# Spectral stages of a Hyena encoder on one Trainium2 core: bins 0 and N1/2 of each request group computed in one step from 64 kept values each, instead of in two steps

## What is computed

```python
def hyena_filters(L, ...):          # both directions of the implicit filter
    k = jnp.concatenate([h[:, 0], jnp.zeros((1, HYENA_ORDER, D_HYENA), f32), h[:0:-1, 1]], axis=0)
    k = k / jnp.sum(jnp.abs(k), axis=0, keepdims=True)
    return jnp.fft.rfft(k, axis=0)

def fft_conv(z, kf, bias):
    L = z.shape[1]
    zf = jnp.fft.rfft(z.astype(jnp.float32), n=2 * L, axis=1)
    y = jnp.fft.irfft(zf * kf, n=2 * L, axis=1)[:, :L]
    return y + z.astype(jnp.float32) * bias.astype(jnp.float32)

z = x1 * fft_conv(v, kf[:, 0], bias[0])
z = x2 * fft_conv(z, kf[:, 1], bias[1])
```

## Time and profile before

| | us |
|---|---|
| median of 3 runs | 2722.59 |
| the 3 runs | 2716.11, 2722.59, 2723.81 |
| the profiled execution, its own time | 2716.53 |
| its span, first to last instruction | 2714.7 |
| spectral stage of order 0, first load to last `gg` | 1326.0 to 1460.0 |
| spectral stage of order 1, first load to last `gg` | 1573.3 to 1707.1 |

### The profile page before, as it was taken

How to read it: one execution, slowest core, us unless ns; L and a number is a source line. 1 busy time by engine, 2 the same in 40 slices (tenths; PEclk the granted TensorE clock), 3 DMA queues, 4 the chain that set the end, 5 groups by cost and what they waited for, 6 DMA issues and landing times. The chain is left out here.

```text
span 2714.7 us, 51042 instructions
## 1 busy us (share of the span) xinstructions
PE 2479.3 (91%) x20059; PEld 1387.5 (51%) x20059; DVE 1905.9 (70%) x2642; ACT 1647.3 (61%) x2326; POOL 1144.4 (42%) x1032
## 2 busy tenths in 40 slices
PE   6899999879999999998898989799954899999997
PEld 4455555426666666663332233354533566666664
DVE  5446767647777777777898989566646577777773
ACT  6634455338888888887655855343434666676651
POOL 1224444226666666667303900244312355444531
PEclk9999999959999999998999989899965899999999
DMA  7413345344411212026796888655543899999972
GB/s 189 129 35 122 115 140 172 117 85 153 114 40 42 47 40 48 25 52 206 256 329 215 292 282 307 198 157 172 156 147 106 263 265 283 264 261 260 275 190 51
DMA packets 392346, 448.05 MB, mean 165 GB/s; under 512 B 205454, under 2 KB 270478, under 8 KB 389840
## 3 DMA queue, kind: packets, MB, share of 16 engines
q1 hardware_dynamic: 367632, 372.73, 45.0%
q0 software_dynamic: 12288, 38.05, 5.9%
q10 hardware_dynamic: 12224, 34.48, 3.7%
HBM read 270.67 MB, written 137.91 MB: 151 GB/s over the span
## 5 line engine op out<-in xcount | busy, mean ns | idle before, releaser
L1254 POOL TENSOR_TENSOR at_p<-at_pf,at_p 128x512 f16<-128x512 f32 x325 | 378.6, 1173 | 263.3 <-ACT at_p L1389 262.9
L1530 DVE TENSOR_REDUCE at_mxs<-at_pM 128x1 f32<-128x512 f32 x512 | 343.9, 688 | 104.6 <-PE at_pM L1420 102.7
L1388 ACT ACTIVATE at_pf<-at_pS,at_scale 128x1024 f32<-128x1024 f32 x260 | 289.8, 1115 | 110.2 <-PE at_pS L1451 105.6
L1389 ACT ACTIVATE at_p<-at_pS,at_scale 128x1024 f16<-128x1024 f32 x260 | 287.8, 1107 | 0.0
L1476 PE MATMUL at_pO<-at_vv,at_p 128*128 128x65 f16 x2080 | 227.0, 194 | 3.1 <-POOL at_p L1254 3.1
L1477 PE MATMUL at_pO<-at_vv,at_p 128*128 128x64 f16 x2080 | 226.4, 195 | 0.0
L1479 PE MATMUL at_pO<-at_vv,at_p 128*128 128x65 f16 x2080 | 225.8, 193 | 0.0
L1420 PE MATMUL at_pM<-at_kT,at_qT 96*128 96x512 f16 x512 | 200.1, 393 | 15.7 <-DMA at_qT<-s_QK 12.5
L1477 PEld LDWEIGHTS at_pO<-at_vv,at_p 128*128 128x128 f16 x2080 | 195.2, 98 | 37.5 <-issue 1.1
L1476 PEld LDWEIGHTS at_pO<-at_vv,at_p 128*128 128x128 f16 x2080 | 195.3, 97 | 35.0 <-issue 3.3
L1449 PE MATMUL at_pS<-at_qT,at_kT 97*128 97x512 f16 (+1 forms) x528 | 202.0, 383 | 3.4 <-DMA at_qT<-at_nmx 2.2
(11 more groups left out here) (423 smaller groups left out, 6237.5 us busy)
## 6 DMA issues: line engine op xcount, KB each, us to landing
sp_rows<-s_F SPq DMA_DIRECT2D x76, 512.0 KB, 5.6
s_F<-fs_a SPq DMA_DIRECT2D x72, 512.0 KB, 3.2
mo_raw<-in_w_gate SPq DMA_DIRECT2D x32, 1024.0 KB
mo_raw<-in_w_up SPq DMA_DIRECT2D x32, 1024.0 KB
mo_down<-in_w_down SPq DMA_DIRECT2D x32, 1024.0 KB, 4.9
s_QK<-pj_R ACTq DMA_DIRECT2D x18, 1024.0 KB, 3.9
s_G<-sp_gg SPq DMA_DIRECT2D x72, 256.0 KB, 4.2
sp_tab<-tab_spec SPq DMA_DIRECT2D x76, 224.0 KB, 4.0
```

What stands on the lines that cost most here:

```text
L1254: eng.tensor_tensor(p2[r][:, half, :], pf[:, r, half, :], p1[r][:, half, :], ALU.subtract).then_inc(own_done if own(g, half) else others_d ...
L1388: act.activation(pf[:, r, :, :], pS[g % 2][:, :, :], ACT.Exp, scale=scale[:, 0:1])
L1389: act.activation(p1[r][:, :, :], pS[g % 2][:, :, :], ACT.Exp, scale=scale[:, 0:1]).then_inc(p_made, 1)
L1530: dve.tensor_reduce(mxs[:, j // NC, j % NC:j % NC + 1], pM[j % 2][:, :], AX.X, ALU.max).then_inc(pM_free, 1)
```

## The change

The two steps of a shared block become one. Of each of the two bins whose rows are real, 64 values of the spectrum are kept: bin 0's 33 real and 31 imaginary values, bin N1/2's 32 and 32; the others are their mirror images. `ends_joined` builds, on the host beside the other tables, one forward table whose 128 columns are the kept values of both bins, and one backward table in which each kept value also carries its mirror image. The two bins need different filter tables. That of bin 0 takes the place of the filter's columns in the joined table, that of bin N1/2 comes as a table `other` of its own for each group, loaded once per order (two transfers of 128 rows of 256 bytes). `cross` shrinks from 128x128 to 128x64. The steps are 36 per order, all alike but for the weights. PE's first matmul now waits for three small tables (`cross_in` at 48), where before it was only the first `cross` matmul that waited, for one.

```diff
+    spec, back, other = ends_joined(spec, back)
...
+def ends_joined(spec, back):
+    h = N2 // 2
+    kept = {0: (np.arange(h + 1), np.arange(1, h)), -1: (np.arange(h), np.arange(h))}
+    twin = {0: lambda k: -k % N2, -1: lambda k: N2 - 1 - k}
...
+    for b in (0, -1):
+        re, im = kept[b]
+        new_spec.append(spec[b][:, np.concatenate([re, N2 + im])])
+        filters.append(spec[b][:, P + np.concatenate([re, im])])
...
+    joined = np.concatenate(new_spec + filters[:1], 1)
+    return np.concatenate([joined[None], spec[1:-1]]), np.concatenate([np.concatenate(new_back)[None], back[1:-1]]), filters[1]
...
-    N0 = NB[0] + 1
-    STEPS = N0 + NB[1] + 1
+    STEPS = sum(NB)
...
-        cross = sb("cross", [P, P])
-        cross_hi = cross[:, :].bitcast(F16)[:, 0:P]
+        cross, other = sb("cross", [P, N2]), sb("other", [P, 2, N2])
+        cross_hi = cross[:, :].bitcast(F16)[:, 0:N2]
+        others = [other[:, g, :].bitcast(F16) for g in range(2)]
...
                 if n == 0:
                     sp.dma_start(cross[:, :], io["tab_cross"]).then_inc(cross_in, 16)
+                    for g in range(2):
+                        sp.dma_start(other[:, g, :], io[f"tab_other{g}"]).then_inc(cross_in, 16)
...
-                over = m == 0
+                ends = m == 0
+                if n == 0:
+                    pe.wait_ge(cross_in, 48)
...
-                        last = pe.matmul(pK[b][out, half, :], w[t][part, P:], x[r][part, 1, :], start=(at == 0),
-                                         stop=(at == 2 and not (over and half == 0)))
-                if over:
-                    if n == 0:
-                        pe.wait_ge(cross_in, 16)
+                        of_k = w[t][part, P:]
+                        if ends and to == 1:
+                            of_k = others[g][part, (w is tab_lo) * H:(w is tab_lo) * H + H]
+                        last = pe.matmul(pK[b][out, half, :], of_k, x[r][part, 1, :], start=(at == 0),
+                                         stop=(at == 2 and not (ends and half == 0 and to == 1)))
+                if ends:
                     for x in (high, low):
-                        last = pe.matmul(pK[b][:, 0, :], cross_hi, x[r][:, 1, :], start=False, stop=(x is low))
+                        last = pe.matmul(pK[b][H:, 0, :], cross_hi, x[r][:, 1, :], start=False, stop=(x is low))
...
             def backward(n):
-                t, c = n % TABS, results[n]
-                out, joins = pG[c % 2], n > 0 and opens(n - 1)
-                if not joins and c >= 2:
-                    pe.wait_ge(g_moved, c - 1)
+                t, out = n % TABS, pG[n % 2]
+                if n >= 2:
+                    pe.wait_ge(g_moved, n - 1)
```

More of the change, by code:

```diff
@@ L81, in dft_tables @@
         spec[b, :, P:] = folded_spectrum(L, b)
+    spec, back, other = ends_joined(spec, back)
     return (first.reshape(2, P, P).transpose(1, 0, 2), last.reshape(2, P, P).transpose(1, 0, 2),
-            np.concatenate([back.astype(np.float32), in_halves(spec)], -1))
+            np.concatenate([back.astype(np.float32), in_halves(spec)], -1), in_halves(other))
+def ends_joined(spec, back):
+    h = N2 // 2
+    kept = {0: (np.arange(h + 1), np.arange(1, h)), -1: (np.arange(h), np.arange(h))}
+    twin = {0: lambda k: -k % N2, -1: lambda k: N2 - 1 - k}
+    new_spec, new_back, filters = [], [], []
+    for b in (0, -1):
+        re, im = kept[b]
+        new_spec.append(spec[b][:, np.concatenate([re, N2 + im])])
+        filters.append(spec[b][:, P + np.concatenate([re, im])])
+        of = back[b].reshape(2, N2, 2, P)
+        sign = np.array([1, -1])
+        re_twin, im_twin = ((twin[b](k) != k)[:, None, None] * of[m, twin[b](k)] * s[None, :, None]
+                            for m, k, s in ((0, re, sign), (1, im, -sign)))
+        new_back.append(np.concatenate([of[0, re] + re_twin, of[1, im] + im_twin]).reshape(N2, 2 * P))
+    joined = np.concatenate(new_spec + filters[:1], 1)
+    return np.concatenate([joined[None], spec[1:-1]]), np.concatenate([np.concatenate(new_back)[None], back[1:-1]]), filters[1]
 TAB_SCALE = 2.0 ** 10
@@ L191, in tables @@
     out["eye"] = np.eye(P)
-    out["cross"] = in_halves(np.repeat(np.arange(P)[:, None] == N2, P, 1))
+    out["cross"] = in_halves(np.repeat(np.arange(P)[:, None] == N2, N2, 1))
     for g, L in enumerate(GROUPS):
-        out[f"first{g}"], out[f"last{g}"], out[f"spec{g}"] = dft_tables(L)
+        out[f"first{g}"], out[f"last{g}"], out[f"spec{g}"], out[f"other{g}"] = dft_tables(L)
         out[f"fold{g}"] = folded_first(L)
@@ L1986, in place @@
         def place(n):
[L1987 to L1994, removed]
+            return (1, n - NB[0]) if n >= NB[0] else (0, n)
         @block.sync
@@ L2103, in backward @@
                     last = pe.matmul(out[:, :], tab[t][:, m * P:(m + 1) * P], pk[n % (LAG + 1)][:, m, :],
-                                     start=(m == 0 and not joins), stop=(m == 1 and not opens(n)))
+                                     start=(m == 0), stop=(m == 1))
                 last.then_inc(g_made, 1)
@@ L2134, in move @@
             def move(n):
-                if n < 0 or opens(n):
+                if n < 0:
                     return
-                c = results[n]
                 dve.wait_ge(g_made, n + 1)
-                if c >= OUTS:
-                    dve.wait_ge(g_out[c % OUTS], 16 * (c // OUTS))
-                dve.tensor_tensor(gg[:, c % OUTS, :], pG[c % 2][:, :], inverse[:, place(n)[0], :], ALU.mult).then_inc(g_moved, 1)
+                if n >= OUTS:
+                    dve.wait_ge(g_out[n % OUTS], 16 * (n // OUTS))
+                dve.tensor_tensor(gg[:, n % OUTS, :], pG[n % 2][:, :], inverse[:, place(n)[0], :], ALU.mult).then_inc(g_moved, 1)
             dve.wait_ge(totalled, 2)
```

12 lines of the change are left out of this document (5 added, 7 removed).

## The result

Seven executions of the changed kernel took 2687.56 to 2704.24 us, median 2699.18. Seven of the kernel before, timed with them, took 2708.23 to 2726.48, median 2716.81. The ratio is 0.9927 with a 95% interval of [0.9904, 0.9949], that is 14 to 26 us less. The profiled execution took 2694.75 us, its span 2693.0.

The account below looks back on a forecast made before the run. The prediction took PE, at 3.24 us a step, to bound the spectral stages. Its terms, -12.96 + 0.4 + 0.8 = -11.8 us, led from a base of 2719.8 to 2708.0 us, range 2702 to 2717.

Parts of the forecast that it names:

- The pace and the steps that go: Both spectral stages: PE sets the pace at 3.24 us a step; four removed steps give 12.96 us less.
- The start: Start of each order: later tables and second block of rows cost PE +0.4 us each, bounds 0 and 1.85.
- The shape of the weights: Steps with `cross`: a second change of weight shape costs 0.10 us, four times, +0.4 us; bounds 0 and +0.8.
- DVE: Spectral steps: every step now has a `gg`, but 3.05 us of DVE work fits in 3.24, so no cost.
- Rival (a): Spectral stages: transfers set the pace, a removed step is worth 2.0 us; -6.8 us, 2713.0; chance 0.08.
- (b): Start of both orders: each pays the upper bound of 1.85 us; -8.9 us, 2710.9; chance 0.07.
- (c): Spectral steps: loads cannot keep up without the light steps; slower needs 3.52 us a step, 2728 us; chance 0.03.
- (d): Merged steps: another pass over the array's quarters costs 2.6 us in four steps; -9.2 us, 2710.6; chance 0.04.
- The sum: Whole kernel: steps, starts and weight shapes together give -11.8 us, between -13.0 and about -8.5.
- the mid-stage wait: Around step 18 of the stage: rows come 2.97 us late for ACT, PE loses about 0.3 us; no change expected.
- How the numbers follow: Whole kernel: faster 0.76, within 0.3% 0.21, slower 0.03; range from 2716.1 - 13.0 less 1 us to 2723.8 - 6.8.
- something outside the two stages moved: Outside the two spectral stages: a sign that the forecast is wrong, if anything there changes; no size given.

Follow-up runs that it names:

- the steps put back: Changed kernel with two plain steps added in each order, 38 steps again: ratio 1.0011 to the kernel before, stages 138.42 and 138.17 us.
- order 1 alone: Kernel before in order 0 (38 steps), changed code and tables only in order 1 (36 steps): ratio 0.9991 to the kernel before, stages 137.20 and 131.24 us.
- the second repeat of the changed kernel: Changed kernel, nothing altered, timed once more against the kernel before: ratio 0.9957, stages 130.52 and 131.79 us.

## Why the prediction was right, and where it was wrong

The measured median, 2699.18 us, lies 2.8 us below the forecast range of 2702 to 2717, while the mechanism came out as forecast. Term by term:

**The pace and the steps that go: right.** 4 x 3.24 us was the term, and rows of after, the steps put back and order 1 alone each give 3.24 a step. No other engine came to set the pace.

**The start: right in kind, too dear.** I took +0.8 us for the two orders. It was 0.05 us in order 0 and 0.17 in order 1 (from first load to first matmul), from one execution each; repeats of either kernel scatter by as much (5.56 to 5.90 us before, 5.61 to 6.07 after). The later issue of the second block cost nothing. The bound of 1.85 for each would have been too low in the wrong place of the queue, where 2.1 and 2.9 were lost.

**The shape of the weights: right**, 0.11 us for each merged step at 2.4 GHz and 0.14 in a cold one, 0.5 against 0.4 forecast. The Trainium skill, TensorEngine Tiling (Array Packing), Key Properties, has the drain at a change of tiling mode; the trace agrees, with 0.10 us as its size.

**DVE and the rivals.** DVE kept up, as said, and had room for one more instruction. Rival (a), the transfers: worth 2.1 us and not 8.0, and only at the start, where one should have looked for it (the earlier trace rows showed the engines full there, and 0.84 busy behind it). Rivals (b), (c) and (d) did not occur. The new tables' rows of 256 bytes were no burden: 3.3 us from issue to landing against 3.5 for `cross` before. The Trainium skill, DMA: Bandwidth & Descriptors, Specifications, asks for at least 512 bytes for line rate; a transfer of 32 KB with rows of 256 bytes shows no cost of that here.

**The sum: -11.8 forecast, -12.6 by the first pair of traces, -13.0 by all stages, -14.1 +- 2.6 by all times.** The mechanism and its size hold. The small remainder is the start, 0.6 us, and the mid-stage wait, which was 0 to 1.3 us from one execution to the next.

**The step that failed is "How the numbers follow".** The range was laid from the four times of before, 2716.1 to 2723.8, as if they bounded the scatter. The 101 executions of the same program went from 2699.9 to 2726.6 us with a mean of 2712.3. The three given and the profiled one all lay above that mean. So both the base of 2719.8 (7.5 us too high) and the low end, 2702, were off: what failed is the choice of the base and the 1 us allowed below the lowest known time, not a term of the change. From 2712.3 the same sum gives 2700.5, and the 13.0 us of the stages 2699.3. I had the sign of this in hand: two pairs of times 6 us apart, in a kernel whose steady rows repeat to 0.01 us, ask for the stage in which executions differ. One profile could not show that. The row to ask about was PE's granted clock outside the changed stages.

**Whether the unchanged parts moved.** The prediction called itself wrong if something outside the two stages moved, and in the first pair of traces 9.1 us did. The three profiled executions of the changed kernel all had a higher clock from 570 to 610 us (0.74, 0.93, 1.00) than the two of the kernel before (0.64, 0.62). Six other kernels with the changed kernel's stages and tables, in whole or nearly, had 0.60, 0.62, 0.64, 0.79, 0.86 and 0.93. The mean granted clock of whole executions decides it: 0.9530 over 94 of the kernel before and 0.9527 over 25 of the changed one. Taking 13 us at full clock out of 2712 at 0.9530 would give 0.9528, so the changed kernel has no higher clock elsewhere, within 0.001 or about 2 us. The higher clocks of its profiled executions were chance.

**What stays open.** That the clock's falling back sets the time ahead of the spectral stages rests on the table (14 executions, nearly in order) and on one kernel in which it was kept up. What makes it fall in one execution and not in another is not shown. Merge and experts scatter by 10 us too (998.4 to 1010.3), and nothing was tried there. The correlation over whole executions says that the clock goes with most of the scatter, not that it causes it.

## What to carry to other kernels

Where one engine was dense at a steady pace, an item removed was worth its pace, and the other engines' share of it was worth nothing; the exception was where another resource was full, here the fill at the start. Before a range is laid around a change of half a per cent, find out how far executions of the unchanged program differ and in which stage: three times do not bound it. Place a new table that the first instruction needs ahead of the bulk loads in the queue; 1.2 us later in the queue, behind the second block, it cost 2 to 3 us.

## What the runs showed of the hardware that was not expected

- PE's granted clock fell back to 1.2 GHz in the midst of dense work and stayed there while PE was 85 to 95% busy, in the kernel before from 574.7 to about 600 us. In the second repeat of the changed kernel it stayed up. What PE did just before does not tell the two apart: in the 10 us ahead of the first score matmul it was busy for 6.04 us in both (first and second line below), and the twelve score matmuls that follow are the same. The one difference seen in the rows is that the clock rose in the twelfth of them in the kernel before and in the tenth in the other. With extra matmuls in that stretch, 8.41 us busy (third line), the clock stayed up, in the one execution profiled.

```profile
556.48:566.48 10.00, 6.04 (x12) 1.05 (x11) 7.08 (x13) 0.00 (x0) 0.00 (x0) 0.50 0.18 39
```

```profile
553.91:563.91 10.00, 6.04 (x11) 1.04 (x11) 7.08 (x13) 0.00 (x0) 0.00 (x0) 0.50 0.18 39
```

```profile
554.86:564.86 10.00, 8.41 (x25) 4.35 (x26) 6.20 (x11) 0.00 (x0) 0.00 (x0) 0.50 0.13 30
```

- A cold clock at the start of a stage was nearly free: raised from 0.50 to 1.00 in the first two steps, it gave 0.3 and 0.6 us, with the DMA engines busy for 1.00 of those steps and PE for 3.74 of 6.10 us.
- Two small transfers in SP's queue delayed the next issue by 0.95 us and the landing hardly at all, with the DMA engines full: ACT could start on the second block 6.81 us behind the stage's first load instead of 7.09 in order 0, and 7.15 instead of 6.95 in order 1.
